# Four layer norms in one Trainium2 kernel: six of eight mean subtractions on GpSimd, half of the affine tiles on VectorE

## The reference, cut to what matters

```python
def layer_norm(x, g, b):
    xf = x.astype(jnp.float32)
    mu = jnp.mean(xf, -1, keepdims=True)
    var = jnp.mean(jnp.square(xf - mu), -1, keepdims=True)
    return ((xf - mu) * lax.rsqrt(var + LN_EPS) * g + b).astype(x.dtype)

for i in range(4):
    ...                                  # out = the mixer of layer i
    h = layer_norm(ALPHA * h + out, ln_g[i], ln_b[i])
```

## Time and profile before

| | |
|---|---|
| time, median of three runs | 3486.62 us (3480.51 to 3488.65) |
| the profiled execution's own time | 3484.2 us |
| its span in the profile | 3482.3 us |
| TensorE matmul busy | 3315.0 us (95%) |
| VectorE busy | 2234.0 us (64%) |
| ScalarE busy | 1838.8 us (53%) |
| GpSimd busy | 487.0 us (14%) |

### The profile page before, as it was taken

How to read it: one execution, slowest core, us unless ns; L and a number is a source line. 1 busy time by engine, 2 the same in 40 slices (tenths; PEclk the granted TensorE clock), 3 DMA queues, 4 the chain that set the end, 5 groups by cost and what they waited for, 6 DMA issues and landing times.

```text
span 3482.3 us, 55160 instructions
## 1 busy us (share of the span) xinstructions
PE 3315.0 (95%) x22787; PEld 2943.3 (85%) x22787; DVE 2234.0 (64%) x3054; ACT 1838.8 (53%) x2892; POOL 487.0 (14%) x739
## 2 busy tenths in 40 slices
PE   6899999999899999999999997999998999899997
PEld 2588888878688999999999886888888998799996
DVE  1787776542545455676666666666666555799866
ACT  1344433332456744777666445555546564678644
POOL 0011111101000000000000013777120000222002
PEclk9999999999999999999999999999999999999999
DMA  9654556632234555555554555666554434455454
GB/s 382 233 197 171 183 197 214 213 113 97 78 124 134 168 179 180 185 179 183 173 190 152 181 182 173 207 205 204 180 182 141 141 132 158 158 170 168 156 181 145
DMA packets 164520, 608.44 MB, mean 175 GB/s; under 512 B 20688, under 2 KB 20720, under 8 KB 162480
## 3 DMA queue, kind: packets, MB, share of 16 engines
q1 hardware_dynamic: 135072, 495.54, 41.9%
q0 software_dynamic: 28624, 107.29, 9.0%
q10 hardware_dynamic: 576, 2.10, 0.2%
HBM read 596.27 MB, written 8.57 MB: 174 GB/s over the span
## 4 chain that ended last, share of the span: by engine, by line
PE 77%; ACT 7%; DMA 7%; DVE 7%; issue 3%; SPq 0%; ACTq 0%; DVEq 0%
PE psum_all L538 22%; PE psum_all L534 16%; PE psum_all L536 16%; PE psum_all L531 11%; DMA raw<-in_stream 5%; ACT w_hi L466 2%; DMA mod_early<-in_stream 2%; DVE w_lo L473 1%; PE psum_all L1375 1%; PE psum_all L1405 1%; ACT ssd_seg L2126 1%; PE psum_all L763 1%; DVE ln_d L1035 1%; PE psum_all L681 1%; DVE act_parts L931 1%
## 5 line engine op out<-in xcount | busy, mean ns | idle before, releaser
L538 PE MATMUL psum_all<-act_parts,w_lo 128*128 128x256 f32 (+1 forms) x6704 | 2009.4, 300 | 0.0
L473 DVE TENSOR_TENSOR w_lo<-raw,w_hi 128x1024 fp32r<-128x1024 f32 x866 | 1066.0, 1244 | 879.1 <-ACT w_hi L466 877.6
L534 PE MATMUL psum_all<-act_parts,w_hi 128*128 128x256 f32 (+1 forms) x4464 | 1407.7, 315 | 48.0 <-DVE act_parts L931 34.0
L536 PE MATMUL psum_all<-act_parts,w_hi 128*128 128x256 f32 (+1 forms) x4464 | 1380.5, 309 | 0.0
L466 ACT ACTIVATE w_hi<-raw 128x1024 fp32r<-128x1024 f32 x866 | 907.9, 1056 | 816.6 <-DMA raw<-in_stream 815.4
L538 PEld LDWEIGHTS psum_all<-act_parts,w_lo 128*128 128x128 f32 x6704 | 1283.6, 191 | 42.2
L534 PEld LDWEIGHTS psum_all<-act_parts,w_hi 128*128 128x128 f32 x4464 | 858.9, 192 | 107.7 <-issue 51.7
L536 PEld LDWEIGHTS psum_all<-act_parts,w_hi 128*128 128x128 f32 x4464 | 859.6, 193 | 43.8 <-issue 3.2
L531 PE MATMUL psum_all<-act_parts,w_hi 128*128 128x512 f32 x2240 | 799.8, 401 | 29.9 <-DVE w_lo L473 15.0
L531 PEld LDWEIGHTS psum_all<-act_parts,w_hi 128*128 128x128 f32 x2240 | 422.6, 189 | 137.4 <-issue 16.1
L782 DVE SCALAR_TENSOR_TENSOR xT<-mod_late,small,xT 128x1024 f32<-128x1024 f32 x210 | 256.3, 1278 | 4.1 <-DMA mod_late<-in_stream 1.7
(11 more groups left out here) (486 smaller groups left out, 3425.8 us busy)
## 6 DMA issues: line engine op xcount, KB each, us to landing
raw<-in_stream SPq DMA_DIRECT2D x866, 512.0 KB, 3.3
mod_late<-in_stream POOLq DMA_DIRECT2D x128, 512.0 KB, 4.5
mod_early<-in_stream SPq DMA_DIRECT2D x64, 512.0 KB, 8.9
ssd_seg<-acs_rows POOLq DMA_DIRECT2D x8, 1536.0 KB, 6.8
s_matrices<-s5p_made POOLq DMA_DIRECT2D x16, 384.0 KB, 3.9
s_made<-s_matrices POOLq DMA_DIRECT2D x16, 256.0 KB, 3.0
xT<-in_x SPq DMA_DIRECT2D x1, 2048.0 KB, 16.2
ctxT<-in_ctx SPq DMA_DIRECT2D x1, 2048.0 KB, 20.6
```

Source lines behind the costliest of these rows:

```text
L473: dve.tensor_tensor(w_lo[:, n % RING, :], raw[:, n % RING, :], w_hi[:, n % RING, :].bitcast(F32), ALU.subtract).then_inc(lo_ready, 1)
L534: pe.matmul(sums, w_hi[:, n % RING, cols], block.rhs(kk, HIGH, block.width), start=(kk == 0), stop=False)
L536: pe.matmul(sums, w_hi[:, n % RING, cols], block.rhs(kk, LOW, block.width), start=False, stop=False)
L538: last = pe.matmul(sums, w_lo[:, n % RING, cols], block.rhs(kk, HIGH, block.width), start=False, stop=(kk == block.kt - 1))
```

## The change

In each of the four norms, `shift` of pairs 2 to 7 is issued on GpSimd (`begin_gpsimd`), at the head of its queue in the stage, behind a wait for the mean; pairs 0 and 1 stay on VectorE. The mean signals through a semaphore of its own. `scale` of these pairs waits for GpSimd. Of each pair's two affine tiles the second goes to VectorE (`whole_vector`), directly behind the pair's scale and a wait for it. The last norm gets a queue on GpSimd too, and SyncE waits for both engines' affine tiles.

```diff
@@ -609,6 +609,8 @@
             def gpsimd(pool):
                 if late:
                     late_loads(pool)
+                if before:
+                    before.begin_gpsimd(pool)
                 if gpsimd_side:
                     gpsimd_side(pool)
                 for r in range(KT + 1) if behind else ():
@@ -890,6 +892,9 @@
             def begin_vector(self, dve, split):
                 pass
 
+            def begin_gpsimd(self, pool):
+                pass
+
         class Affine(Hand):
 
 
@@ -967,11 +972,14 @@
                 self.centred, self.squared = signal("ln_centred", KT), signal("tiles_squared", KT)
                 self.means, self.vars, self.spread = signal("ln_means", 1), signal("tiles_summed", 1), signal("ln_spread", 1)
                 self.rooted = signal("tiles_rooted", 1)
-                self.shifted, self.scaled = signal("ln_shifted", KT // 2), signal("tiles_scaled", KT // 2)
+                self.mean_made = signal("ln_mean_made", 1)
+                self.shifted, self.scaled = signal("ln_shifted", 2), signal("tiles_scaled", KT // 2)
+                self.shifted_too = signal("ln_shifted_by_gpsimd", KT // 2 - 2)
 
                 self.at = {10: (0, 4), 11: (4, 8), 12: (8, 12), 13: (12, 13), 14: (13, 14), 15: (14, 15)}
                 self.affine([(xT[:, k:k + 2, :], [(param("ln_g", n * KT + i, n * KT + i + 1),
-                                                   param("ln_b", n * KT + i, n * KT + i + 1), "act") for i in (k, k + 1)],
+                                                   param("ln_b", n * KT + i, n * KT + i + 1),
+                                                   "act" if i == k else "dve") for i in (k, k + 1)],
                               pair_of(act_hi, 0, k), pair_of(act_lo, 0, k)) for k in range(0, KT, 2)])
                 self.out = out
 
@@ -1055,14 +1063,20 @@
                     act.wait_ge(self.scaled.sem, self.scaled.at(p + 1))
                 self.make_parts(act, ready, split, self.out)
 
-            def shift(self, dve, p):
+            def shift(self, eng, p, done):
                 x = xT[:, 2 * p:2 * p + 2, :]
-                dve.tensor_tensor(x, x, self.mean[:, :].unsqueeze(1).broadcast_to([P, 2, T]), ALU.subtract) \
-                   .then_inc(self.shifted.sem, 1)
+                eng.tensor_tensor(x, x, self.mean[:, :].unsqueeze(1).broadcast_to([P, 2, T]), ALU.subtract) \
+                   .then_inc(done.sem, 1)
+
+            def begin_gpsimd(self, pool):
+                pool.wait_ge(self.mean_made.sem, self.mean_made.at(1))
+                for p in range(2, KT // 2):
+                    self.shift(pool, p, self.shifted_too)
 
             def scale(self, dve, p):
                 x = xT[:, 2 * p:2 * p + 2, :]
-                dve.wait_ge(self.shifted.sem, self.shifted.at(p + 1))
+                dve.wait_ge(*((self.shifted.sem, self.shifted.at(p + 1)) if p < 2 else
+                              (self.shifted_too.sem, self.shifted_too.at(p - 1))))
                 dve.tensor_tensor(x, x, norm_root[:, :].unsqueeze(1).broadcast_to([P, 2, T]), ALU.mult) \
                    .then_inc(self.scaled.sem, 1)
 
@@ -1072,8 +1086,8 @@
 
                 dve.wait_ge(self.means.sem, self.means.at(1))
                 dve.scalar_tensor_tensor(out=self.mean[:, :], in0=self.half[:, :], scalar=0.5, in1=self.sums[1],
-                                         op0=ALU.mult, op1=ALU.add).then_inc(ordered.sem, 1)
-                dve.wait_ge(ordered.sem, ordered.step())
+                                         op0=ALU.mult, op1=ALU.add).then_inc(self.mean_made.sem, 1)
+                dve.wait_ge(self.mean_made.sem, self.mean_made.at(1))
                 dve.tensor_tensor(self.off[:, :], self.mean[:, :], self.half[:, :], ALU.subtract).then_inc(ordered.sem, 1)
                 dve.wait_ge(ordered.sem, ordered.step())
                 dve.tensor_tensor(self.off[:, :], self.off[:, :], self.off[:, :], ALU.mult).then_inc(ordered.sem, 1)
@@ -1081,7 +1095,7 @@
                 dve.wait_ge(self.vars.sem, self.vars.at(1))
                 dve.tensor_tensor(norm_root[:, :], self.var, self.off[:, :], ALU.subtract).then_inc(self.spread.sem, 1)
                 for p in range(2):
-                    self.shift(dve, p)
+                    self.shift(dve, p, self.shifted)
                 dve.wait_ge(self.rooted.sem, self.rooted.at(1))
                 dve.reciprocal(norm_root[:, :], norm_root[:, :]).then_inc(ordered.sem, 1)
                 dve.wait_ge(ordered.sem, ordered.step())
@@ -1089,8 +1103,8 @@
                 for p in range(pieces + 1):
                     if p < pieces:
                         self.scale(dve, p)
-                    if p + 2 < pieces:
-                        self.shift(dve, p + 2)
+                        dve.wait_ge(self.scaled.sem, self.scaled.at(p + 1))
+                        self.whole_vector(dve, p)
                     if p >= 2 and self.out:
                         self.make_low(dve, p - 2)
                     split(p)
@@ -3215,7 +3229,7 @@
                  gpsimd_side=gpsimd_side)
         s5()
         stage(tensor=norms[3].begin_tensor, scalar=lambda act: norms[3].begin_scalar(act, lambda i: None),
-              vector=lambda dve: norms[3].begin_vector(dve, lambda i: None))
+              vector=lambda dve: norms[3].begin_vector(dve, lambda i: None), gpsimd=norms[3].begin_gpsimd)
 
 
         @block.sync
@@ -3238,7 +3252,8 @@
                 n[kind] = m + 1
 
             for c in range(4):
-                sp.wait_ge(norms[3].whole["act"].sem, norms[3].whole["act"].at(4 * c + 4))
+                for engine in ("act", "dve"):
+                    sp.wait_ge(norms[3].whole[engine].sem, norms[3].whole[engine].at(2 * c + 2))
                 sp.dma_start(out[:, 4 * c:4 * c + 4, :], xT[:, 4 * c:4 * c + 4, :]).then_inc(written, 16)
             sp.wait_ge(written, 64)
             sp.wait_ge(stage_done, 4 * stage_count[0])
```

## The result

The changed kernel takes 3494.27 us (median of 20 runs, 3487.28 to 3500.83) against 3484.92 us of the kernel before (20 runs, 3479.2 to 3490.16). The forecast was 13 us slower. Single runs of either kernel spread over more than 10 us, so in what follows the time tells whether, and the moments inside a norm tell where: counted from M, the end of the mean, they repeat within 0.1 us from norm to norm and from kernel to kernel.

A forecast was written before the change was run, and what follows sets the result against it. TensorE was taken to bound the kernel, waiting in the norms for VectorE's low halves. Three inner norms at 3.3 us plus 3.0 in the last gave +13 on the 3486.6 us median: 3499.6 us, range 3491 to 3509.

The forecast's parts named there:

- the turns: In the norms, GpSimd reads and two-input VectorE instructions hold each other up whole; five turns of 1.16 us stall VectorE.
- rival (4): TensorE's clock behind the fourth pair: less half-rate work gives 3496.6 us, more gives 3505.6; chance 0.22, half each way.
- rival (3): Cheaper turns in the norms: square not two-input, or affine tile doesn't wait; +11.6 us, both +10.5; 0.55 together with forecast.
- Rival (1): In the norms, no turns or turns that hit only GpSimd: -4.2 us, 3482.4 us; chance 0.10.
- Rival (2): GpSimd's subtractions in the norms take 1.71 us, every turn 0.41 longer: +23 us, 3509.6 us; chance 0.13.
- the low half of rival (4): In each norm 2 us less at half rate behind the fourth pair, 1 us back: +10, 3496.6 us; chance 0.11.
- The moves at no cost: GpSimd's S5 DMA issues and a position load before MLA go behind the norm's subtractions; claimed to cost nothing.

The follow-up runs named there:

- the one with GpSimd's writes: Kernel before plus sixteen GpSimd memsets (128x352) after the mean in each norm, into a buffer nobody reads; one timed run, 3493.34 us.
- the one with one subtraction: Kernel before with only the last pair's subtraction on GpSimd, behind a wait for the root, beside the reciprocal; one timed run, 3487.22 us.
- the first order: Kernel before with VectorE's and ScalarE's queues reordered, two affine tiles of the last norm on VectorE; ratio 0.9987.
- both orders: The first order, 0.9987; and another with GpSimd's last-pair subtraction, one VectorE affine tile per inner norm and later weight units, 0.9984; both against the kernel before.
- the late start: Changed kernel with GpSimd's six subtractions behind a wait for the root instead of the mean alone; one timed run, 3490.89 us.

## Why the prediction was right

**The direction and the mechanism.** The forecast rested on the turns of the earlier trace rows, and they are there. By its own steps, from M: the square to 1.90 (measured 1.86), the second subtraction to 5.32 (5.20), the reciprocal from 5.24 (5.12), the first multiplication to 8.28 (8.10), the first low half to 12.42 (12.06), the fourth to 17.40 (17.01), the last norm's last affine tile to 17.3 (16.89). The forecast time was 3499.6 and 3494.27 was measured; 1.7 of the difference lies in the kernel before, whose median of 20 runs is 3484.92, not the 3486.62 that the sum was put on.

**What was mis-sized.** A turn behind GpSimd was put at 1.16, interpolated from a 256 column addition. The end of the two subtractions on VectorE gives it: 5.20 = 1.86 + 2 x 0.55 + 2 turns, so 1.12, with the forecast's 0.55 for VectorE's part. The first affine tile ends 0.15 after GpSimd lets go, not 0.26 (2095.76 against 2086.47 + 9.14 = 2095.61). And the loop's step is 1.65, not 1.66. Together these are 0.4 in each norm, 13 down to 11.4. The rest, 11.4 to 10.1, is inside the interval, and smaller than what the clock may have given back (rival (4) below). How near the total comes is luck in that part, since the sum gave the clock nothing. The lower end of the range, 3491, is 5.6 below rival (4)'s 3496.6, not some 4.

**Which of VectorE's instructions are held.** The square of one tensor was (1.37), so rival (3) is out in that half. The variance, with one input in PSUM, and the reciprocal were not (0.42 and 1.74). The affine tile was: 1.24 instead of 0.41, as the earlier trace rows had it for a tensor_scalar, so the other half of (3) is out as well. The Trainium skill, page SBUF — State Buffer, section "Who interferes with whom", counts tensor_scalar among the operations that can take the shared ports; the 1.24 bears it out here.

**Rival (1), no turns or only for GpSimd.** VectorE's subtractions never took less than 1.30. Out. **Rival (2), 1.71 a subtraction.** The least was 1.26. Out: repeating the mean's index cost nothing. The rival rested on a misread row, for L1161's 1.71 was never GpSimd's own time. VectorE's and GpSimd's timelines in the kernel before, at one of its fourteen additions:

```profile
803.53 1.23 DVE L473 TENSOR_TENSOR w_lo<-raw,w_hi 128x1024 fp32r<-128x1024 f32 x1 [2.22 <-ACT w_hi L466]
...
804.19 1.72 POOL L1161 TENSOR_TENSOR layer_acc<-layer_acc,layer_sq 128x512 f32<-128x512 f32 x1 [9.05 <-ACT layer_sq L1152]
```

GpSimd starts 0.66 into a two-input VectorE instruction and ends 1.15 after its end; the other thirteen lie just the same. That is the turn itself, for the very size that the forecast interpolated to 1.16.

**Rival (4), the clock.** What counts is TensorE's work at half rate behind the fourth pair, since from there on it is busy nearly throughout. In the changed kernel 2.4 GHz is back by then: over the 6 us behind the fourth low half the granted clock was 1.00, 1.00 and 0.97 in the three inner norms. In the kernels whose fourth low half ends at M + 14.07 it often was not back: 1.00, 1.00, 0.81 in the kernel before, 0.76, 0.65, 0.68 in the one with GpSimd's writes, 0.85, 1.00, 0.65 in the one with one subtraction. The third norm of the changed kernel, of the one with GpSimd's writes, and of the one with the subtractions alone (the columns as in the earlier trace rows, over 6 us):

```profile
3023.75:3029.75 6.00, 5.49 (x43) 5.23 (x42) 5.93 (x10) 4.75 (x9) 0.00 (x0) 0.97 0.42 134
...
3029.64:3035.64 6.00, 5.94 (x35) 5.94 (x36) 5.45 (x9) 5.88 (x11) 0.00 (x0) 0.68 0.25 87
...
3039.87:3045.87 6.00, 5.94 (x34) 5.94 (x35) 5.45 (x9) 5.88 (x11) 0.00 (x0) 0.64 0.26 87
```

The nine norms that run as before have 0.82 on average, which loses 6 x 0.18 = 1.1 us; the changed kernel's three lose 0.1. By this estimate the clock gave back about 1 us in each inner norm, as the low half of rival (4) had it, and 11.4 would become some 8.4. With the subtractions alone (0.56, 0.59, 0.64) and the affine tiles alone (0.66, 0.52, 0.57) it took about 1.4 more a norm than in the nine, which would put 4 us on their 11.7 and 10.1; 15.7 and 13.3 were measured. Each kernel has one profiled execution, the norms of one kernel differ by up to 2 us in this, and each interval holds both sums. So that the clock makes the difference between the moments and the times is argued, not shown.

With the first order the clock over these 6 us was 0.75, 0.96 and 0.77, on average what the nine have. So nothing there says that the earlier pairs were lost to the clock; why it brought 4.5 and not 5.5 stays open, and the interval can't tell them apart.

**The moves at no cost.** GpSimd's transfers of the S5 stage went behind the subtractions, from 3003.68 to 3015.90; the matmul that reads them did not wait:

```profile
3006.82 9.13 POOL L1068 TENSOR_TENSOR xT<-xT,ln_mean 128x512 f32<-128x512 f32 x6 [5.16 <-DVE ln_mean L1088]
3015.90 0.56 POOL L3174 DMA_DIRECT2D s_b_re<-in_s_b_re  x1
...
3031.52 0.27 PE L2960 MATMUL psum_all<-consts,s_b_re 128*128 128x128 f32 x1
```

It starts at M + 24.8, M being 3006.74; before, at M + 21.7: 3.1 later, the norm's own delay of 2.95 and a little.

**What a single pair of profiles can't show.** From the last M back to the first the two profiled executions differ by 6 us, not by 3 x 2.95. The kernels whose norms run as before differ among themselves by as much there: the kernel with GpSimd's writes has 1382.7 from the first M to the last, the one before 1373.2. The times need many runs; the moments inside a norm don't.

## What to carry to other kernels

An idle engine isn't free help: before giving GpSimd a share of VectorE's work, look in the trace for a row where the two overlap, and price the move by what VectorE loses (here five turns of 1.12 in a norm, for six instructions of 0.60). If GpSimd is to help, put its reads beside instructions that were not held here, such as the reciprocal or one with an input in PSUM (a tensor_scalar was held, though it reads one tensor), and make sure that the engine relieved was the late one; when VectorE was relieved of 0.60 it waited 0.59 for ScalarE. Reordering a fixed queue by what the consumer needs first, with two affine tiles moved, brought 4.5 us (1.0 to 8.4) where moving work between engines alone lost 10 or brought next to nothing. The moments of both orders could be laid out beforehand to 0.2 us from the durations and start-to-start steps of one trace. Count the queues of all engines that feed the consumer: the one forecast that counted VectorE's alone was 0.6 off.

## What the runs showed of the hardware that was not expected

- GpSimd and VectorE take strict turns under load, also across kinds of instruction: with six reads queued on one and multiplications and affine tiles on the other, each got every second turn, and a later start of GpSimd only moved the stretched rows (1.24, 1.75, 1.23, 1.74 in the late start).
- A 128x512 subtraction with the mean repeated took GpSimd 1.26 at least, no more than plain additions at L1017 (1.30). A GpSimd duration in a trace can hold a wait that no bracket shows: all of L1161's 1.71 begin 0.66 into a VectorE instruction of 1.23.
- How much TensorE does at half rate behind the fourth pair differs from norm to norm of one kernel: over 6 us the granted clock was 1.00, 1.00 and 0.81 in the kernel before. The change and its two halves, which move the same pairs by 2.6 to 3.1 us, had 0.99, 0.60 and 0.58 there on average.
